# Another VectorE order at the ends of both attentions of a diffusion backbone, one latent projection between the last softmaxes, and the path weights rounded one block sooner

## Chip, cores and metric

One Trainium2 chip, one core. The metric is the device time of one launch in microseconds (us), the median of several runs. PE is TensorE, DVE is VectorE, ACT is ScalarE, POOL is GpSimd, and SP is the queue that starts nearly all loads.

## What is computed

Two layers (`DEPTH` = 2) over 640 tokens: 512 latent ones and 128 context ones, width 1024. The reference, cut to what matters here:

```
proj = h @ w_in[l]                    # hyena 1536, q k v 512 each, latent q 384, kv 256, kr 32, paths 1536, merge 3072
pr = softmax(s, -1); pr = pr[:, 0] - lam * pr[:, 1]          # differential attention (DA), 4 heads
y_da = rms_norm(pr @ v, da_subln) * (1 - lam_init)
c_q, c_kv = rms_norm(mla_dq), rms_norm(mla_dkv)              # the latent projections
y_mla = softmax(q k^T) v                                     # latent attention (ML), 8 heads
br = [y_hy, y_da, y_mla] * silu(paths)
merged = sum over the 3 branches of sigmoid(merge) * (br @ w_branch)
x = layer_norm(ALPHA * x + gate * (merged @ w_out))
```

## The kernel before

Everything runs in an order written by hand. `STEPS[l]` is one list of steps per layer, and every engine walks the same list and does its own part of each step, so each engine is in order. A step's result in PSUM goes to one of four slots of 1024 columns, dealt round in the order of the list. A step that takes a slot waits until the result that was in it, four slot uses earlier, has been read: those are the waits `freed`.

A *projection* is one step (`dqkv`, `path`, `mgate`, `v`, ...): a tile of 128 weight columns times all 640 tokens. The tile is split: ACT copies it from `W` to `Wh` (rounded, `high_part`), POOL, or for some tiles DVE, writes the rest into `Wl` (`low_part`), and PE runs 32 matmuls with `Wh` (lines 817 and 818) and 16 with `Wl` (822). `Wh` has two buffers, `W` has three. The table `UPTO` says at which step ACT and POOL do the rounding of a tile. With `near` true the tile that follows tile n is rounded at the start of tile n's own step, that is ahead of ACT's reading of tile n's result; with `near` false it is done at the next step, after that reading.

An attention is a run of units u = (head, block of 128 queries), five units a head, the fifth for the context tokens with a single block of 128 keys. For a unit PE computes scores (`da_score` into two slots, line 1073; `ml_score`, line 902 or 900), DVE takes the maximum (1525), ACT the exponential (1375 or 1449), DVE the normalised weights (`da_weights`, lines 1532 to 1535; `ml_weights`, 1552 and 1553). Two units later (`LAG` = 2) `ptrans` transposes the weights on PE (878), ACT copies them, and after a head's last unit `pv` multiplies with the values (923 and 924; 920 and 924 for ML). Weights of unit u-1 are written by DVE in the step `score` u, behind the maximum of unit u; those of an attention's last unit, in the step of the last `ptrans`. Projections are put between the units as *fillers*: here `mgate` d and `mbranch` d, at whose end DVE reads the result (1775, or 1778 and 1779).

After each DA head come `dasq` h (DVE squares the head's output, 1831), `dams` h (PE sums it over the 128 rows, 865; DVE scales the sum, 1836). After the last head `dart` (ACT square root, DVE reciprocal) and `dab` 0 to 3 (PE spreads the row, 873; DVE multiplies, 1845) finish the norm. The latent projections `dqkv` 0 to 4 stand among them; DVE squares each (1853), `mms` 0 sums the squares of the first three (865, DVE scales with 1871) and `mms` 1 the other two. The square of `dqkv` 3 overwrites that of `dqkv` 0, so DVE waits there for `mms` 0.

SP runs ahead of everybody as far as its waits let it. At step `dqkv` 3 it waits for the sum of the last head, since the weights that come next overwrite its input, then starts four loads of the latent attention and only then tile `dqkv` 3:

```
if (kind, i) == ("dqkv", 3):
    sp.wait_ge(*filled(l, "dams", 3))
    for dst, src in (wuq, wukv, cc, ckr):      # 1152, 1024, 128 and 16 KB
        sp.dma_start(dst, src)
...
weight(TILE_AT[l, kind, i] + n)                # 512 KB, waits for w_lo of the tile three before
```

Of the kernel before, what the change touches and what calls it, by code (L numbers as in the profile page):

```python
# [18 lines left out]
KD = D // 128  # L19
NT = NTOK // 128  # L20
# [3 lines left out]
DAH, DHD, DAV = 4, 64, 128  # L24
MH, MN, MR, MV = 8, 64, 32, 64
# [34 lines left out]
LAG = 2  # L60


def attention_steps(tag, heads, fillers, before=None, behind=None, full=False):


    steps, units, taken = [], [(h, t) for h in range(heads) for t in range(NT)], 0
    for u, (h, t) in enumerate(units):
        if before and h + 1 < heads:
            steps += before(h + 1, t)
        steps.append((tag + "_score", u))  # L70
        if u > LAG and (u - LAG - 1) % NT == NT - 1:
            steps.append((tag + "_pv", (u - LAG - 1) // NT))
        if behind and u > LAG + 1 and (u - LAG - 2) % NT == NT - 1:
            steps += behind((u - LAG - 2) // NT)[:1]
        if behind and u > LAG + 2 and (u - LAG - 3) % NT == NT - 1:
            steps += behind((u - LAG - 3) // NT)[1:]
        upto = min(t, 3) + 1 + 4 * h if full else len(fillers) * (u + 1) // len(units)
        steps += fillers[taken:upto]
        taken = upto
        if u >= LAG:  # L80
            steps.append((tag + "_ptrans", u - LAG))
    return steps + [(tag + "_ptrans", len(units) - LAG + n) for n in range(LAG)] + [(tag + "_pv", heads - 1)]


def path_steps(n):
# [3 lines left out]
def merge_steps(n):  # L89
    return [(kind, KD * n + d) for d in range(KD) for kind in ("mgate", "mbranch")]  # L90
# [47 lines left out]
def layer_steps(l):  # L138
# [25 lines left out]
        if c:  # L164
            s += [("vt", c - 1)]
    s += [("vt", 3)]
    s += attention_steps("da", DAH, merge_steps(0), behind=lambda h: [("dasq", h), ("dams", h)], full=True)
    s += [("dasq", 3), ("dqkv", 0), ("dams", 3), ("dqkv", 1), ("dart", 0), ("dqkv", 2)] + [("dab", h) for h in range(DAH)]
    s += [("dqkv", 3), ("mms", 0), ("dqkv", 4), ("kr", 0), ("mms", 1)]
    p = path_steps(1)  # L170
    s += p[:1] + [("mrt", 0)] + p[1:3] + [("mb", 0), ("mb", 1)] + p[3:] + [("cc", 0), ("sc", 0)]
    s += [("mv", i) for i in range(3)]
# [170 lines left out]
SLOT = slot_table()  # L343


def upto_table():


    table = {}
    for l in range(DEPTH):  # L350
        steps = [(n, step) for n, step in enumerate(STEPS[l]) if step[0] not in ("gmod", "nmod", "cload", "mload")]
        places = [n for n, (_, step) in enumerate(steps) if step in SPLIT_AT]
        table[l, STEPS[l].index(("ht", 0))] = 2
        for n, (a, b) in list(enumerate(zip(places, places[1:])))[1:]:
            near = b - a <= 2 or (SPLIT[n][0] == "conv" and b - a <= 3) or SPLIT[n] == ("qk", 0)
            table[l, steps[a if near else a + 1][0]] = n + 2
        table[l, STEPS[l].index(("inv", 4))] = SPLIT_AT["qk", 2] + 1
        early = SPLIT_AT["conv", 8]
        table[l, STEPS[l].index(("conv", 6))] = early + 1
    return table  # L360
# [62 lines left out]
def build(nc, A, O):  # L423
# [10 lines left out]
    with ctx:  # L434
# [189 lines left out]
        def after(name, l, count):  # L624

            return sems[name], l * PER[name] + count
# [6 lines left out]
        def filled(l, kind, i, j=0):  # L633

            s, u, _ = SLOT[l, kind, i, j]
            return full[s], u + 1
# [863 lines left out]
        def _(dve):  # L1500
# [27 lines left out]
            def da_weights(l, u):  # L1528

                n, s, e = keysn(u), st[:, u % (LAG + 1)], E[u % (LAG + 1)]  # L1530
                dve.wait_ge(*after("da_exp", l, 2 * u + 2))
                link(dve.reciprocal(s[:, 4:6], s[:, 2:4]))
                link(TT(s[:, 6:7], s[:, 5:6], lamc[:, 6:7], ALU.mult))
                link(TS(e[:, 0, 0:n], e[:, 0, 0:n], s[:, 4:5], None, ALU.mult))
                STT(e[:, 0, 0:n], e[:, 1, 0:n], s[:, 6:7], e[:, 0, 0:n], ALU.mult, ALU.add).then_inc(sems["da_p"], 1)
                dve.wait_ge(*own("da_p"))
# [48 lines left out]
            for l in range(DEPTH):  # L1585
                for kind, i in STEPS[l]:
# [9 lines left out]
                    elif kind in ("gmod", "nmod"):  # L1596
                        n = MODS[l].index((kind, i))
# [168 lines left out]
                    elif kind == "mbranch":  # L1766
                        n_, d = divmod(i, KD)
                        g = 12 * n_ + 4 + d
                        dve.wait_ge(*filled(l, kind, i))
                        ps = slot(l, kind, i)  # L1770
                        dve.wait_ge(*after("th_ready", l, g + 1))
# [46 lines left out]
                    elif kind == "da_score":  # L1818
# [5 lines left out]
                            dve.wait_ge(*own("da_max"))  # L1824
                        if i:
                            da_weights(l, i - 1)
                    elif kind == "da_ptrans" and i == DAH * NT - 1:
                        da_weights(l, i)
                    elif kind == "dasq":
                        dve.wait_ge(*after("da_o", l, i + 1))  # L1830
                        TT(sqd[:, i % 2], OT[:, i], OT[:, i], ALU.mult).then_inc(sems["da_sq"], 1)
# [46 lines left out]
                    elif kind == "mb":  # L1878
# [4 lines left out]
                        last.then_inc(sems["c_ready"], 1)  # L1883
                        dve.wait_ge(*own("c_ready"))
                    elif kind == "mqr":
                        dve.wait_ge(*after("mqr_raw", l, i + 1))
                        link(dve.stream_shuffle(qsw, rq, mask=[p ^ 8 for p in range(32)]))
                        TT(rq, rq, rope_m[:, 0], ALU.mult)
# [6 lines left out]
                    elif kind == "ml_score":  # L1895
                        dve.wait_ge(*filled(l, kind, i))
                        softmax_max(slot(l, kind, i), keysn(i), st[:, i % (LAG + 1), 0:1]).then_inc(sems["ml_max"], 1)
                        dve.wait_ge(*own("ml_max"))
                        if i:
                            ml_weights(l, i - 1)  # L1900
                    elif kind == "ml_ptrans" and i == MH * NT - 1:
                        ml_weights(l, i)
                    elif kind in ("xt", "xta", "xtb"):
                        dve.wait_ge(*filled(l, kind, i))
                        ps, blocks = slot(l, kind, i), BLOCKS[kind]
# [186 lines left out]
```

## Time and profile before

| | |
|---|---|
| median of 3 runs | 1925.25 us (1922.32 to 1926.27) |
| profiled execution | 1925.0 us, of it span 1923.2 us |
| PE busy (matmul) | 1802.9 us, 94% |
| DVE busy | 1125.5 us, 59% |
| ACT busy | 670.4 us, 35% |
| POOL busy | 451.7 us, 23% |
| chain that ended last | PE 66%, DVE 23%, issue 4%, ACT 4%, DMA 2%, POOL 1% |
| TensorE clock granted, mean | 0.983 of full speed |

Busy is the share of the span in which an engine executes; the chain is followed back from the last instruction to what released each one. A bracket behind a row of the timeline is the time the engine was idle ahead of it, and what ended that. Layer 0's DA ends near 490 us and its ML near 790 us; layer 1's, 938 us later.

### The profile page before, as it was taken

The numbers are of one execution on the slowest core, as the hardware profiler recorded it, in microseconds if no ns is written. First come the engines' busy times: TensorE is split into PE (matmuls) and PEld (weight loads), VectorE is DVE, ScalarE is ACT, GpSimd is POOL, SyncE is SP. The second block draws the span as 40 slices with busy tenths as digits, with TensorE's granted clock in tenths as the row PEclk, the third lists the DMA queues.
The fourth block names the chain that finished last, engine by engine and source line by source line (L and its number), as shares of the span: only waits on it lengthen the run. The fifth ranks groups of instructions, "written<-read, shape, count | busy, mean of one in ns | idle before, by whom it ended". The sixth has DMA issues, their size and how long they took to land.

```text
span 1923.2 us, 27833 instructions
## 1 busy us (share of the span) xinstructions
PE 1802.9 (94%) x11336; PEld 1572.3 (82%) x11336; DVE 1125.5 (59%) x1606; ACT 670.4 (35%) x1159; POOL 451.7 (23%) x208
## 2 busy tenths in 40 slices
PE   4999999999999999999989999999999999999997
PEld 3788799877786777899876969997879677779996
DVE  4689894445343444377877989925434343434755
ACT  3434312434234444321263342234433344442222
POOL 0100033222231111367300001322122211115561
PEclk8999999999999999999999999999999999999999
DMA  8111122211210111353621112221122011014431
GB/s 347 44 55 34 33 89 71 60 40 51 105 50 26 34 34 39 114 198 115 245 88 33 56 33 78 77 61 46 38 72 99 22 37 33 30 48 142 164 111 66
DMA packets 48622, 150.01 MB, mean 78 GB/s; under 512 B 9386, under 2 KB 11050, under 8 KB 47728
## 3 DMA queue, kind: packets, MB, share of 16 engines
q1 hardware_dynamic: 44896, 134.09, 20.3%
q10 hardware_dynamic: 3600, 14.16, 2.2%
q8 instruction: 90, 1.47, 0.3%
q14 instruction: 36, 0.29, 0.0%
HBM read 141.63 MB, written 6.59 MB: 77 GB/s over the span
## 4 chain that ended last, share of the span: by engine, by line
PE 66%; DVE 23%; issue 4%; ACT 4%; DMA 2%; POOL 1%; SPq 0%; ACTq 0%; DVEq 0%; POOLq 0%
PE PS L817 15%; PE PS L818 14%; PE PS L822 14%; PE PS L889 4%; PE PS L878 3%; PE PS L1140 2%; PE PS L923 2%; PE PS L920 2%; PE PS L1073 2%; PE PS L902 2%; DVE MG L1779 1%; DVE Wl L1546 1%; DVE st L1525 1%; DMA pmod_w<-in_w_mod 1%; PE PS L1129 1%
## 5 line engine op out<-in xcount | busy, mean ns | idle before, releaser
L1958 POOL TENSOR_TENSOR Wl<-W,Wh 128x1024 fp32r<-128x1024 f32 (+1 forms) x156 | 350.3, 2247 | 1291.9 <-ACT Wh L1193 1234.7
L817 PE MATMUL PS<-Hh,Wh 128*128 128x320 f32 x2048 | 613.5, 314 | 20.8 <-ACT Wh L1193 12.3
L818 PE MATMUL PS<-Hl,Wh 128*128 128x320 f32 x2048 | 604.9, 310 | 0.0
L817 PEld LDWEIGHTS PS<-Hh,Wh 128*128 128x128 f32 x2048 | 386.7, 189 | 45.9 <-issue 29.0
L818 PEld LDWEIGHTS PS<-Hl,Wh 128*128 128x128 f32 x2048 | 386.8, 189 | 0.6 <-issue 0.5
L822 PE MATMUL PS<-Hh,Wl 128*128 128x320 f32 x2048 | 321.4, 309 | 0.9 <-POOL Wl L1958 0.9
L822 PEld LDWEIGHTS PS<-Hh,Wl 128*128 128x128 f32 x2048 | 305.5, 188 | 1.5 <-POOL Wl L1958 1.5
L1525 DVE TENSOR_REDUCE st<-PS 128x1 f32<-128x640 f32 (+1 forms) x160 | 114.8, 718 | 315.1 <-PE PS L902 172.7
L1193 ACT ACTIVATE work<-PS 128x640 f32<-128x640 f32 (+9 forms) x298 | 172.6, 592 | 250.6 <-PE PS L822 64.2
L1193 ACT ACTIVATE Wh<-W 128x1024 fp32r<-128x1024 f32 (+1 forms) x188 | 176.4, 943 | 62.0 <-PE PS L822 26.8
L1350 ACT ACTIVATE th<-PS 128x640 f32<-128x640 f32 x64 | 45.1, 705 | 366.0 <-PE PS L822 366.0
L1193 ACT ACTIVATE raw<-PS 128x320 f32<-128x320 f32 (+4 forms) x98 | 38.1, 443 | 261.0 <-PE PS L822 188.6
L817 PE MATMUL PS<-BRh,Wh 128*128 128x320 f32 x384 | 116.4, 317 | 0.0
L818 PE MATMUL PS<-BRl,Wh 128*128 128x320 f32 x384 | 113.4, 309 | 0.0
L878 PE MATMUL PS<-fixed,work 128*128 128x128 f32 x580 | 88.5, 285 | 18.4 <-ACT work L1495 5.0
L878 PEld LDWEIGHTS PS<-fixed,work 128*128 128x128 f32 x580 | 72.7, 153 | 39.3 <-issue 12.8
L902 PE MATMUL PS<-work 96*128 96x320 f32 x256 | 81.0, 441 | 7.8 <-DVE MG L1779 4.5
L1604 DVE SCALAR_TENSOR_TENSOR raw<-work 128x1024 f32<-128x1024 f32 x46 | 82.4, 1792 | 7.6 <-DMA work<-in_w_mod_rows 6.1
L817 PEld LDWEIGHTS PS<-BRh,Wh 128*128 128x128 f32 x384 | 72.1, 188 | 7.0 <-ACT Wh L1193 6.1
L1375 ACT ACTIVATE work<-PS,st 128x640 f32<-128x640 f32 (+1 forms) x80 | 56.7, 710 | 55.7 <-DVE st L1525 55.7
L818 PEld LDWEIGHTS PS<-BRl,Wh 128*128 128x128 f32 x384 | 72.2, 188 | 0.0
L889 PE MATMUL PS<-work,MG 128*128 128x512 f32 x160 | 70.8, 594 | 1.0 <-ACT raw L1193 0.6
(234 smaller groups left out, 2502.8 us busy)
## 6 DMA issues: line engine op xcount, KB each, us to landing
W<-in_w_in SPq DMA_DIRECT2D x132, 512.0 KB, 3.5
W<-in_w_branch SPq DMA_DIRECT2D x48, 256.0 KB, 2.6
work<-in_w_mod_rows ACTq DMA_DIRECT2D x23, 512.0 KB, 3.7
pmod_w<-in_w_mod SPq DMA_DIRECT2D x8, 1024.0 KB, 14.4
W<-in_w_out SPq DMA_DIRECT2D x16, 512.0 KB, 4.5
work<-in_x_sample SPq DMA_DIRECT2D x2, 2048.0 KB
late_modulation_w<-in_w_mod_rows SPq DMA_DIRECT2D x5, 512.0 KB, 6.6
x_mid<-work SPq DMA_DIRECT2D x1, 2560.0 KB, 8.5
```

The lines of the kernel that those rows point to most:

```text
L817: pe.matmul(out, Wh[:, b, kk, :], xh[:, kk, t], start=kk == 0, stop=False)
L818: pe.matmul(out, Wh[:, b, kk, :], xl[:, kk, t], start=False, stop=False)
L822: last = pe.matmul(out, Wl[:, b, kk, :], xh[:, kk, t], start=False, stop=kk == k - 1)
L878: return pe.transpose(out, in_, ident[0:p, 0:p])
L889: last = pe.matmul(ps[:, 512 * q:512 * q + HY], table, srcs[q ^ c][:, r, :], start=n_ == 0, stop=n_ == len(terms) - 1)
L902: last = pe.matmul(ps[:, 512 * a:512 * a + HALF], q_lat[:, 128 * t:128 * t + 128], k[:, HALF * a:HALF * a + HALF], start=True, stop=True)
L1193: return act.activation(out, in_, ACT.Copy, scale=scale)
L1350: act.activation(halves(th[:, n % 2]), two(ps), ACT.Tanh, scale=0.5)\
L1375: act.activation(two_or_one(e, n), two(ps) if n > CTX else ps[:, 0:n], ACT.Exp, bias=st[:, i % (LAG + 1), j:j + 1], accum_out=st[:, i % (L ...
L1525: return dve.tensor_reduce(out, two(ps) if n > CTX else ps[:, 0:n], mybir.AxisListType.XY if n > CTX else AX, ALU.max, negate=True)
L1604: ins = STT(mod_early if n < EARLY[l] else mod_late, modw[mod_buffer(l, n)], scale, cb[:, j], ALU.mult, ALU.mult, accum_out=modcs[:, at_ % ...
L1958: return pool.tensor_tensor(out, in_, high.bitcast(f32), ALU.subtract)
```

## The change

Five edits. (1) In DA, `dasq` h goes behind the filler of its unit, and `dams` h one unit later, behind that unit's score. (2) `cover`: `dqkv` 0, and `dams` 2 behind it, go between the third-last and the second-last `ptrans` of DA; every later `dqkv` moves up by one place, and `dqkv` 3 and `mms` 0 go ahead of the four `dab`. (3) DVE writes the weights of DA's last unit in the last `score` step. (4) In ML, DVE writes the last unit's weights ahead of `mbranch` 15, and those of unit 14 ahead of the rotation of the second group of queries (`mqr` 1). (5) `early_high` makes `near` true for `path` 4 to 7, `dqkv` 0 and `dqkv` 3. The number of instructions of each engine is the same.

```
-        if behind and u > LAG + 1 and (u - LAG - 2) % NT == NT - 1:
-            steps += behind((u - LAG - 2) // NT)[:1]
-        if behind and u > LAG + 2 and (u - LAG - 3) % NT == NT - 1:
-            steps += behind((u - LAG - 3) // NT)[1:]
+        if behind and u > LAG + 3 and (u - LAG - 4) % NT == NT - 1:
+            steps += behind((u - LAG - 4) // NT)[1:]
         upto = min(t, 3) + 1 + 4 * h if full else len(fillers) * (u + 1) // len(units)
         steps += fillers[taken:upto]
         taken = upto
+        if behind and u > LAG + 1 and (u - LAG - 2) % NT == NT - 1:
+            steps += behind((u - LAG - 2) // NT)[:1]
         if u >= LAG:
             steps.append((tag + "_ptrans", u - LAG))
-    return steps + [(tag + "_ptrans", len(units) - LAG + n) for n in range(LAG)] + [(tag + "_pv", heads - 1)]
+    return steps + list(cover) + [(tag + "_ptrans", len(units) - LAG + n) for n in range(LAG)] + [(tag + "_pv", heads - 1)]
...
-    s += attention_steps("da", DAH, merge_steps(0), behind=lambda h: [("dasq", h), ("dams", h)], full=True)
-    s += [("dasq", 3), ("dqkv", 0), ("dams", 3), ("dqkv", 1), ("dart", 0), ("dqkv", 2)] + [("dab", h) for h in range(DAH)]
-    s += [("dqkv", 3), ("mms", 0), ("dqkv", 4), ("kr", 0), ("mms", 1)]
+    s += attention_steps("da", DAH, merge_steps(0), behind=lambda h: [("dasq", h), ("dams", h)], full=True,
+                         cover=[("dqkv", 0), ("dams", 2)])
+    s += [("dasq", 3), ("dqkv", 1), ("dams", 3), ("dqkv", 2), ("dart", 0), ("dqkv", 3), ("mms", 0)] + [("dab", h) for h in range(DAH)]
+    s += [ ("dqkv", 4), ("kr", 0), ("mms", 1)]
...
+def early_high(tile):
+    return tile[0] == "path" and 4 <= tile[1] < 8 or tile in (("dqkv", 0), ("dqkv", 3))
...
-            near = b - a <= 2 or (SPLIT[n][0] == "conv" and b - a <= 3) or SPLIT[n] == ("qk", 0)
+            near = b - a <= 2 or (SPLIT[n][0] == "conv" and b - a <= 3) or SPLIT[n] == ("qk", 0) or early_high(SPLIT[n])
...
                     elif kind == "mbranch":
+                        if i == 2 * KD - 1:
+                            ml_weights(l, MH * NT - 1)
...
-                    elif kind == "da_ptrans" and i == DAH * NT - 1:
-                        da_weights(l, i)
+                        if i == DAH * NT - 1:
+                            da_weights(l, i)
...
                     elif kind == "mqr":
+                        if i:
+                            ml_weights(l, 3 * NT - 1)
...
-                        if i:
+                        if i and i != 3 * NT:
                             ml_weights(l, i - 1)
-                    elif kind == "ml_ptrans" and i == MH * NT - 1:
-                        ml_weights(l, i)
```

DVE at the border of two DA heads: `MG` is the reading of `mbranch`, the row `work<-work 128x640` on line 1831 (1839 in the changed kernel) is `dasq`, `raw<-PS` is `dams`. Before:

```order
L1535 SCALAR_TENSOR_TENSOR work<-work,st 128x640
L1831 TENSOR_TENSOR work<-work 128x640
L1775 SCALAR_TENSOR_TENSOR MG<-th,PS 128x640
L1525 TENSOR_REDUCE st<-PS 128x1 x2
L1532 RECIPROCAL st<-st 128x2
L1533 TENSOR_TENSOR st<-st,small 128x1
L1534 TENSOR_SCALAR work<-work,st 128x640
L1535 SCALAR_TENSOR_TENSOR work<-work,st 128x640
L1836 TENSOR_SCALAR raw<-PS 64x320
L1525 TENSOR_REDUCE st<-PS 128x1 x2
```

And with the change:

```order
L1541 SCALAR_TENSOR_TENSOR work<-work,st 128x640
L1783 SCALAR_TENSOR_TENSOR MG<-th,PS 128x640
L1839 TENSOR_TENSOR work<-work 128x640
L1531 TENSOR_REDUCE st<-PS 128x1 x2
L1538 RECIPROCAL st<-st 128x2
L1539 TENSOR_TENSOR st<-st,small 128x1
L1540 TENSOR_SCALAR work<-work,st 128x640
L1541 SCALAR_TENSOR_TENSOR work<-work,st 128x640
L1531 TENSOR_REDUCE st<-PS 128x1 x2
```

The square and the reading of the filler have changed places, and the scaling has left the place between two softmax units; it now follows the weights of the next unit.

ACT from the end of DA on. `Wh_56<-W_55 128x1024` is the rounding of a tile, `work_76<-PS` with a number is the copy of a result (640 columns wide: of `pv` 3 or of a `dqkv`), the table load and `raw_63` are the square root of `dart`. Before, from the copy of `pv` 3:

```order
L1193 ACTIVATE work_76<-PS2 128x640
L1193 ACTIVATE Wh_56<-W_55 128x1024
L1193 ACTIVATE work_76<-PS3 128x640
L1193 ACTIVATE Wh_56<-W_55 128x1024
L1193 ACTIVATE work_76<-PS1 128x640
L1395 ACT_TABLE_LOAD
L1395 ACTIVATE raw_63<-raw_63 128x640
L1193 ACTIVATE work_76<-PS2 128x640
L1193 ACTIVATE Wh_56<-W_55 128x1024 x2
L1193 ACTIVATE work_76<-PS3 128x640
```

With the change, from the same copy:

```order
L1199 ACTIVATE work_76<-PS3 128x640
L1199 ACTIVATE Wh_56<-W_55 128x1024
L1199 ACTIVATE work_76<-PS0 128x640
L1199 ACTIVATE Wh_56<-W_55 128x1024
L1199 ACTIVATE work_76<-PS2 128x640
L1401 ACT_TABLE_LOAD
L1401 ACTIVATE raw_63<-raw_63 128x640
L1199 ACTIVATE Wh_56<-W_55 128x1024
L1199 ACTIVATE work_76<-PS3 128x640
```

The results copied between the roundings were `dqkv` 0, 1, 2, 3 and are now `dqkv` 1, 2, 3; the second rounding shown is of tile `dqkv` 2 before and of tile `dqkv` 3 now, and it stands ahead of the copy of `dqkv` 2 and of the square root.

DVE at the end of ML, where `th<-th,PS` and `MG<-MG,th` are the reading of `mbranch` 15. Before:

```order
L1552 RECIPROCAL st<-st 128x1
L1553 TENSOR_SCALAR raw<-raw,st 128x640
L1778 SCALAR_TENSOR_TENSOR th<-th,PS 128x640
L1779 TENSOR_TENSOR MG<-MG,th 128x640
L1552 RECIPROCAL st<-st 128x1
L1553 TENSOR_SCALAR work<-work,st 128x128
```

With the change:

```order
L1558 RECIPROCAL st<-st 128x1
L1559 TENSOR_SCALAR raw<-raw,st 128x640
L1558 RECIPROCAL st<-st 128x1
L1559 TENSOR_SCALAR work<-work,st 128x128
L1786 SCALAR_TENSOR_TENSOR th<-th,PS 128x640
L1787 TENSOR_TENSOR MG<-MG,th 128x640
```

The two instructions that write the last unit's weights now come ahead of the filler's result.

## Rows read from the trace of the kernel before

**Rows 1.** What PE waited for, whole span: total us, times, longest

```profile
PE PS L865 <- DVE MG L1775: 4.6, 6, 0.8
...
PE PS L878 <- DVE work L1553: 4.2, 2, 2.1
```

**Rows 2.** Timeline, border of DA heads 2 and 3: start, us, work [idle before]

```profile
442.29 0.37 ACT L1375 ACTIVATE work<-PS,st 128x128 f32<-128x128 f32 x1 [0.81 <-DVE st L1525]
...
443.28 1.35 PE L1073 MATMUL PS<-work 64*128 64x320 f32 x8
...
445.44 0.38 PE L817 MATMUL PS<-Hh,Wh 128*128 128x320 f32 x1 [0.81 <-DVE raw L1836]
```

**Rows 3.** Timeline of PE and ACT, end of DA, layer 0

```profile
459.56 4.56 PE L923 MATMUL PS<-work 128*128 128x512 f32 x10
...
477.39 0.49 PE L1073 MATMUL PS<-work 64*128 64x128 f32 x4
...
481.54 0.77 PE L878 MATMUL PS<-fixed,work 128*128 128x128 f32 x5 [1.46 <-DVE work L1535]
...
482.34 0.70 ACT L1193 ACTIVATE work<-PS 128x640 f32<-128x640 f32 x1 [1.52 <-PE PS L878]
...
483.53 0.28 ACT L1193 ACTIVATE work<-PS 128x128 f32<-128x128 f32 x1 [0.48 <-PE PS L878]
...
483.86 6.19 PE L923 MATMUL PS<-work 128*128 128x512 f32 x10 [0.37 <-ACT work L1193]
...
490.03 0.39 PE L817 MATMUL PS<-Hh,Wh 128*128 128x320 f32 x1
...
497.24 0.73 PE L865 MATMUL PS<-work,fixed 128*32 128x320 f32 x4
```

**Rows 4.** Timeline of SP, layer 0, as it passes the wait at `dqkv` 3

```profile
498.01 0.38 SPq L759 DMA_DIRECT2D work<-in_mla_w_uq  x1
...
500.18 0.46 SPq L675 DMA_DIRECT2D W<-in_w_in  x1
```

**Rows 5.** That tile's DMA, layer 0, then layer 1: size, us from issue to landing

```profile
W<-in_w_in SPq DMA_DIRECT2D x1, 512.0 KB, 8.7
...
W<-in_w_in SPq DMA_DIRECT2D x1, 512.0 KB, 7.5
```

**Rows 6.** Timeline from the four `dab` to `mms` 0, layer 0

```profile
513.94 1.80 DVE L1845 SCALAR_TENSOR_TENSOR work<-work,small,PS 128x640 f32<-128x640 f32 x2
...
514.97 0.61 PE L817 MATMUL PS<-Hh,Wh 128*128 128x320 f32 x1 [1.10 <-ACT Wh L1193]
...
523.50 1.81 PE L865 MATMUL PS<-work,fixed 128*32 128x320 f32 x12
```

**Rows 7.** Timeline around `path` 7 and the values of ML, layer 0

```profile
563.84 0.42 PE L817 MATMUL PS<-Hh,Wh 128*128 128x320 f32 x1 [0.99 <-ACT Wh L1193]
...
569.26 2.61 PE L822 MATMUL PS<-Hh,Wl 128*128 128x320 f32 x16 [0.47 <-POOL Wl L1958]
...
572.51 1.05 ACT L1193 ACTIVATE Wh<-W 128x1024 fp32r<-128x1024 f32 x1
...
574.33 10.57 PE L1129 MATMUL PS<-work 128*128 128x512 f32 x24 [1.74 <-ACT work L1193]
```

**Rows 8.** Timeline of PE, ML: `mqn` 2 behind `ptrans` 14, then `pv` 7 in both layers

```profile
669.20 3.51 PE L1140 MATMUL PS<-work 128*128 128x512 f32 x12
...
788.47 2.38 PE L920 MATMUL PS<-work 128*64 128x256 f32 x20 [0.37 <-ACT work L1193]
...
1727.02 3.65 PE L920 MATMUL PS<-work 128*64 128x256 f32 x20 [0.37 <-ACT work L1193]
```

**Rows 9.** Stretches: busy us of PE, PEld, DVE, ACT, POOL, then granted clock

```profile
484.00:490.00 6.00, 6.00 (x12) 2.62 (x13) 0.00 (x0) 0.00 (x0) 0.00 (x0) 0.74 0.00 0
...
981.00:986.00 5.00, 4.42 (x21) 4.21 (x22) 2.09 (x4) 2.22 (x5) 0.00 (x0) 0.55 0.78 328
```

**Rows 10.** Timeline of PE, start of layer 1: the longest wait inside the span

```profile
981.56 4.30 PE L878 MATMUL PS<-fixed,work 128*128 128x128 f32 x20 [5.03 <-ACT work L1495]
```

More of the change, by code:

```diff
@@ L60, with attention_steps @@
 LAG = 2
-def attention_steps(tag, heads, fillers, before=None, behind=None, full=False):
+def attention_steps(tag, heads, fillers, before=None, behind=None, full=False, cover=()):
     steps, units, taken = [], [(h, t) for h in range(heads) for t in range(NT)], 0
```

## The prediction

> **What bounds the kernel now.** I read the shares first, then the waits of PE, then the timeline at each place that the diff touches. PE is busy 1802.9 of 1923.2 us, so all other waits together leave it idle some 120 us, and the chain that ended last lies on PE for 66% and on DVE for 23%. No instruction is removed. What can change is only when PE stands still, and at which of its two clock levels it works. The waits of PE list the places: `dams` (line 865) waited six times, 4.6 us in all, for DVE's reading of a filler, and the single transpose of a context unit's weights twice, 2.1 us at the longest [rows 1]. The timeline shows the rest: at a DA border `mgate` waits 0.81 us for the scaling of `dams` [rows 2]; at the end of DA PE stands 1.46, then 0.85, then 0.37 us between transposes and values (the 0.85 is what is left between the rows at 481.54 and 483.86), and the ten value matmuls that follow take 6.19 us where the same ten took 4.56 a head earlier [rows 3]. The granted clock of that stretch is 0.74 [rows 9], part of it at 1.2 GHz in place of 2.4: the chain of short waits is paid for a second time by 1.6 us of slow matmuls. `dqkv` 3 has 1.10 us ahead of it [rows 6], `path` 7 has 0.99 and 0.47, the values of ML 1.74 [rows 7], the last `pv` of ML 2.11 and 0.37 [rows 1, 8].
>
> **Part 1: the borders of DA heads (edit 1).** Twice a layer, `dams` 0 and 1. Before, PE lost 0.77 (4.6 over six) ahead of `dams` and 0.81 ahead of `mgate`, 1.58 together [rows 1, 2]. With the change, DVE reads the filler 0.8 us sooner and both these waits are gone. But the slots are dealt anew: the next score (443.28 before) now takes the slot of the context unit's first score, and waits for its exponential, which ACT begins at 442.29, since DVE still does square and maximum in the old time, and which takes 0.4 [rows 2]. PE is ready for that score at about 441.9 (`ptrans` comes in `dams`' place), so it stands 0.9. Score 443.28 becomes 442.8, `dams` follows it (0.65), `mgate` starts at 444.7 in place of 445.44: 0.7 saved, four times: **2.8 us**. Bounds: nothing, if the exponential comes later still by 0.7, and 6.3, if there is no new wait. I take 2.8, because each time in it is a row's.
>
> **Part 2: the end of DA (edits 2, 3, 5).** I follow layer 0. The last score ends at 477.9. Before, `dqkv` 0 started at 490.03 and `dams` 3 at 497.24, so a projection costs 7.2 [rows 3]. Now: `ptrans` 17 to 478.5, `dqkv` 0 to 485.7, under which DVE writes both last units' weights. `dams` 2 and `ptrans` 18 (0.7 each) to 487.1, `ptrans` 19 under ACT's copy, the two copies (0.70, 0.28) to 488.2. The values take 4.5 at full clock, since the one wait left is some 0.8, to 492.7. With `dqkv` 0 done, that is 4.5 ahead of before (497.24). `dqkv` 1 ends at 499.9, `dams` 3 at 500.6.
>
> Here the gain meets SP. Its wait at `dqkv` 3 ended with `dams` 3, at 498.01, and the tile of `dqkv` 3 was issued at 500.18, behind four loads of 2.3 MB [rows 4]. It landed 8.7 us later in layer 0 and 7.5 in layer 1 [rows 5], which is 10.9 us after `dams` 3 (508.9) and, with the same 2.2 us of issue, 9.7 in layer 1. Before, that was hidden: between `dams` 3 and `dqkv` 3 PE had two projections and the spreads, and came to `dqkv` 3 at 514.97 [rows 6]. Now only one projection stands there, `dqkv` 2. It ends at 507.8. The tile lands at 511.5, ACT rounds it and PE starts 1.1 later (the row's wait for `Wh`, nearly all of it the 1.05 of the rounding [rows 6, 7]) at 512.6: **a new wait of 4.8 us, in layer 1 of 3.6.** No edit touches SP's order; rounding earlier can't help a tile that isn't there. Queued behind the rounding on ACT stand the copy of `dqkv` 2 and the square root of `dart`, then the reciprocal on DVE; they are done before PE has finished `dqkv` 3, so I cost them at nothing.
>
> After such a wait PE works slowly. The row for it is the start of layer 1: 5.03 us idle, and then a mean clock of 0.55 over five us [rows 9, 10], some 4.5 us at 1.2 GHz, which cost 2.2. The short waits at the end of DA cost 1.6. I take 1.7, near the short one, since the wait is as long as that row's but PE was in full work up to it: `dqkv` 3 runs 512.6 to 521.5, `mms` 0 (1.81) to 523.3. DVE then does square of `dqkv` 3, scaling of `mms` 0 and the first `dab`: three instructions, the last 0.9 [rows 6], 2.2 together (2.7 at most), before the slots for `dab` 3 and `dqkv` 4 are free. `dqkv` 4 starts at 525.5, before it was 523.50 + 1.81 = 525.3 [rows 6]. So layer 0 loses 0.2, and layer 1, with 1.2 less of a wait, wins 1.0: **0.8 us** for the whole part, nearly all of it eaten. Bounds: if the tile isn't waited for, `dqkv` 3 runs 507.8 to 515.0, `dqkv` 4 starts at 519.0, and the part gives 6.3 a layer, 12.6. If the clock drops a second time at the small waits around `dab`, it gives 0.8 - 2 x (1.5 + 0.3), or -2.8.
>
> A page of the Trainium skill gives another price for the loads. DMA: Bandwidth & Descriptors (Where 436 GB/s comes from; Latency and other measured facts) puts the limit into SBUF near 435 GB/s and a fixed cost near 2 us. The five loads are 2.9 MB, by that page an estimate of 6.7 + 2 = 8.7 us, where the rows show 10.9 and 9.7. By the page the wait would be 2.6 in both layers and the sum 3.2 better. The rows decide: the issue alone takes 2.2 us of it, and they differ by layer.
>
> **Part 3: paths (edit 5).** `path` 6 is followed by the spreads `mb`, so the tile of `path` 7 was rounded only after `path` 6 was read. Now ACT does it under `path` 6, and POOL does `Wl` ahead of the low part of the branch; both waits, 0.99 and 0.47, go. `path` 7 likewise hands its place to `mgate` 8: the rounding (1.05) leaves the gap of 1.74 ahead of the values of ML, 0.7 stays [rows 7]. That is 2.5 a layer, **5.0 us**. All inputs are early: the tiles land a projection or more ahead. Bounds: 2.1 (only the middle one of these edits' waits, 1.05, goes in each layer) and 5.5.
>
> **Part 4: ML (edit 4).** At `mqr` 1 the transpose of unit 14 no longer waits 1.7 us. But the next on PE, `mqn` 2, starts at 669.20 in the slot of unit 15's scores [rows 8], just as their exponential ends, and its maximum stands behind the same rotation as before. PE comes to it earlier and waits longer: **nothing**. At the end of ML the weights of unit 39 fall into time in which DVE waited for the filler. The last transpose follows at once and its wait of 2.11 goes, but its copy now queues on ACT behind those of the two transposes ahead, some 0.4 by the 0.70 of such a copy [rows 1, 3]: 1.7 in layer 0. In layer 1 the same, and `pv` 7 took 3.65 there in place of 2.38 [rows 8]; I count that the slow clock goes with the wait, 1.3: 3.0. Sum **4.7 us**; bounds 3.4 (clock stays) and 5.
>
> **Sum.** 2.8 + 0.8 + 5.0 + 4.7 = 13.3 us off the profiled execution's 1925.0, that is 1911.7. The median of the runs is 1925.25, 0.25 above it: **1912 us**, 0.7% faster.
>
> **Rivals.** (a) *The loads are hidden anyway.* For it: the tile's landing differs by 1.2 us between the layers, and 0.5 MB alone would come sooner. Against: SP is one queue and the four loads stand ahead in code. Then part 2 gives 12.6 and the time is 1925.25 - 25.1 = 1900. Chance 0.15. (b) *The loads go at the page's rate* (the wait is 2.6 twice): 1912 - 3.2 = 1909. The rule is that of the DMA page above. Chance 0.08; traces don't bear it out. (c) *The clock takes more.* Two drops a layer, part 2 at -2.8, and part 1 gives nothing: 13.3 - 3.6 - 2.8 = 6.9, 1918. For it: one wait of five us, then spreads of one row with two waits of half a us, just where PE ran slowly in the trace of before. Chance 0.14. TensorE: Matmul & The Clock Gate (HAM oscillation) describes this: a wait for a DMA in the middle of a loop puts the array back to the low clock, and the cost is half of the throttled time. (d) *The tile of `dqkv` 3 comes much later, and the kernel is slower.* Each us costs one in each layer, so it decides from 6.7 us on (a landing 17.6 after `dams` 3 in layer 0). At 8 later: 1912 + 16 = 1928. Against it, 10.9 and 9.7 in the rows. With anything else that ends above 1921: 0.06. (e) *The change does as the sum says*, 1907 to 1917: 0.57.
>
> **Range and chances.** 1900 to 1919 holds (e), (b), (c) and about half of (a); what is left out is (d), half of (a) and the far end of (c), 0.17. A measurement of this kernel tells about 0.2%, 3.9 us, from no change. Faster than 1921.4: 0.88. Within: 0.07. Slower: 0.05.
>
> **What would show it.** In the changed trace: PE's waits for DVE at line 865 and at the 1.46 and 0.85 gone; the first score of DA heads 2 and 3 waiting near 0.9 for ACT's exponential; the values of DA at 4.6 us; `dqkv` 3 waiting 4.8 and 3.6 us for `Wh`, with ACT waiting for the DMA of `W` ahead of it, and low clock behind; no wait at `path` 7, 0.7 at the values of ML; the transpose at `mqr` 1 without a wait and `mqn` 2 with 1.9; `pv` 7 of ML 1.7 sooner. I am wrong if `dqkv` 3 doesn't wait (then nearer 1900), or if PE's clock falls at other places too.

## The result, and the profile after

The changed kernel takes 1930.66 us (median of 5 runs, 1929.99 to 1932.94), the one before 1923.82 beside it (1922.32 to 1926.27): the ratio is 1.0037, 95% interval 1.0022 to 1.0051. That is 0.4% slower, where 1912 us, 0.7% faster, was forecast.

The profiled execution took 1932.48 us, its span 1930.7, 7.5 more than before. Two lines of the page after, the busy times and the chain's shares by engine:

```profile
PE 1805.9 (94%) x11336; PEld 1576.2 (82%) x11336; DVE 1138.2 (59%) x1606; ACT 668.8 (35%) x1159; POOL 447.1 (23%) x208
...
PE 69%; DVE 20%; ACT 4%; issue 3%; DMA 3%; SPq 0%; POOL 0%; ACTq 0%; DVEq 0%
```

DVE executes the same instructions as before and is busy 12.7 us longer (1125.5 before): some of them last longer. That is the first sign. The waits of PE after (total us, times, longest):

```profile
PE PS L823 <- ACT Wh L1199: 15.3, 12, 4.0
...
PE PS L1079 <- ACT work L1381: 9.8, 6, 2.3
...
PE PS L879 <- DVE work L1879: 4.7, 2, 2.3
...
PE PS L926 <- DVE MG L1787: 3.1, 2, 1.6
```

`dams` no longer waits for `MG` [rows 1]. In its place stand the score behind a context unit (line 1079, 2.3 us), tile `dqkv` 3 (line 823, 4.0), `dab` 3 (line 879, 2.3) and the last `pv` of ML (line 926, 1.6). The timeline of the changed kernel at the border that [rows 2] show of before:

```profile
443.37 2.35 POOL L1966 TENSOR_TENSOR Wl<-W,Wh 128x1024 fp32r<-128x1024 f32 x1 [3.00 <-PE PS L828]
443.40 0.82 DVE L1783 SCALAR_TENSOR_TENSOR MG<-th,PS 128x640 f32<-128x640 f32 x1
...
444.26 2.15 DVE L1839 TENSOR_TENSOR work<-work 128x640 f32<-128x640 f32 x1
...
446.44 0.62 DVE L1531 TENSOR_REDUCE st<-PS 128x1 f32<-128x128 f32 x2
446.82 0.37 ACT L1381 ACTIVATE work<-PS,st 128x128 f32<-128x128 f32 x1 [2.24 <-DVE st L1531]
...
447.42 1.35 PE L1079 MATMUL PS<-work 64*128 64x320 f32 x8 [2.32 <-ACT work L1381]
```

The square of `dasq` (line 1839) takes 2.15 us, and ends 0.7 after GpSimd's subtraction has ended (443.37 + 2.35 = 445.72). The reading of `mbranch` ahead of it (line 1783: one input in PSUM) lies under the same subtraction and takes its 0.82. The maximum, the exponential and the score all come behind the square. And the timeline of the same square and subtraction before:

```profile
440.19 0.82 DVE L1831 TENSOR_TENSOR work<-work 128x640 f32<-128x640 f32 x1
440.26 2.97 POOL L1958 TENSOR_TENSOR Wl<-W,Wh 128x1024 fp32r<-128x1024 f32 x1 [2.99 <-PE PS L822]
...
525.34 2.41 POOL L1958 TENSOR_TENSOR Wl<-W,Wh 128x1024 fp32r<-128x1024 f32 x1 [6.62 <-ACT Wh L1193]
525.46 2.96 DVE L1853 TENSOR_TENSOR work<-work 128x640 f32<-128x640 f32 x1 [7.88 <-PE PS L865]
```

There the square of `dasq` began 0.07 us ahead of the subtraction and it was GpSimd that took 2.97 in place of 2.4. The other pair shows the reverse: the square of `dqkv` 3 began 0.12 behind GpSimd and took 2.96. So the trace of before held both cases, and the prediction read neither.

The end of DA in the changed kernel, tile `dqkv` 3 and then the `dab`, layer 0:

```profile
504.57 0.38 SPq L765 DMA_DIRECT2D work<-in_mla_w_uq  x1
...
506.77 1.43 SPq L681 DMA_DIRECT2D W<-in_w_in  x3
...
514.15 1.06 ACT L1199 ACTIVATE Wh<-W 128x1024 fp32r<-128x1024 f32 x1 [9.54 <-DMA W<-in_w_in]
...
515.26 0.64 PE L823 MATMUL PS<-Hh,Wh 128*128 128x320 f32 x1 [3.50 <-ACT Wh L1199]
...
526.78 2.34 POOL L1966 TENSOR_TENSOR Wl<-W,Wh 128x1024 fp32r<-128x1024 f32 x1 [5.54 <-ACT Wh L1199]
526.91 2.90 DVE L1861 TENSOR_TENSOR work<-work 128x640 f32<-128x640 f32 x1 [4.39 <-PE PS L871]
529.84 0.48 DVE L1879 TENSOR_SCALAR work<-PS 64x320 f32<-64x320 f32 x1
...
530.37 0.88 PE L879 MATMUL PS<-raw,fixed 1*128 1x320 f32 x4 [2.34 <-DVE work L1879]
```

The forecast wait for the late tile is there, 3.50 us (4.8 forecast) and 3.96 in layer 1 (3.6). Behind it comes a second one: `dab` 3 needs the slot that DVE frees with the scaling of `mms` 0, and that stands behind a square of 2.90 us. Windows of the changed kernel (PEclk, third from the right, is the mean granted clock) over the borders and the end of DA in both layers:

```profile
400.00:550.00 150.00, 138.24 (x838) 116.04 (x835) 70.53 (x104) 52.17 (x95) 33.64 (x17) 0.95 0.19 68
1340.00:1480.00 140.00, 127.90 (x749) 105.83 (x750) 67.63 (x99) 48.31 (x92) 30.07 (x15) 0.93 0.20 68
```

and of the kernel before:

```profile
400.00:550.00 150.00, 142.16 (x885) 120.63 (x884) 68.95 (x111) 54.10 (x96) 36.34 (x17) 0.98 0.20 71
1340.00:1480.00 140.00, 132.16 (x815) 110.50 (x814) 61.15 (x100) 50.10 (x92) 33.38 (x16) 0.98 0.21 72
```

A mean of 1.00 is 2.4 GHz and one of 0.50 is 1.2 GHz, so in layer 1 the mean of 0.93 over 140 us is 2 x 0.07 x 140 = 20 us at 1.2 GHz, where 0.98 was 6. The clock fell behind most of the new waits, but not behind each. Windows of the changed kernel, first in layer 0 and then in layer 1: behind the score's wait at one of the two borders, and behind the wait for tile `dqkv` 3:

```profile
447.00:451.00 4.00, 3.58 (x23) 2.56 (x24) 3.72 (x9) 2.31 (x8) 0.00 (x0) 1.00 0.14 53
514.00:521.00 7.00, 5.74 (x22) 5.75 (x23) 5.07 (x2) 4.61 (x5) 4.50 (x2) 0.52 0.50 186
...
1350.00:1354.00 4.00, 4.00 (x18) 2.62 (x15) 3.64 (x8) 1.74 (x4) 0.00 (x0) 0.57 0.02 4
1456.00:1463.00 7.00, 5.15 (x20) 5.15 (x21) 4.48 (x2) 4.61 (x5) 3.91 (x2) 0.51 0.53 198
```

The other two borders have 0.57 (408 to 412) and 0.61 (1388 to 1392), and behind the `dab` 3 wait it is 0.58 (531 to 535) and 0.51 (1473 to 1480). The same score, after the same 2.32 us, kept the full clock in one place of four. `mqn` 2 of ML shows it once more, 12 matmuls behind a wait of 2.07 us, in layer 0 and in layer 1 (timeline of the changed kernel):

```profile
673.94 5.21 PE L1146 MATMUL PS<-work 128*128 128x512 f32 x12 [2.07 <-ACT work L1455]
...
1617.77 3.51 PE L1146 MATMUL PS<-work 128*128 128x512 f32 x12 [2.07 <-ACT work L1455]
```

So the length of a wait of some 2 us does not tell here whether the clock falls behind it; what decides that, no run here shows.

**The theory** is then two causes, each with its share of the clock: (i) VectorE instructions such as the square, with both inputs in SBUF, that begin while GpSimd subtracts are held until it ends; (ii) the tile of `dqkv` 3 is late. The rivals: the redealt slots or the clock alone; and that the parts of the change harm or feed each other. The Trainium skill, page SBUF — State Buffer (SBUF: two separate sides), states (i) as a rule: a VectorE instruction in a two-port mode, or one with two inputs in SBUF while GpSimd's instruction reads SBUF, and the GpSimd instruction exclude one another for the whole length of whichever began first. The rows agree in both directions: VectorE's 0.82 us became 2.96, and GpSimd's 2.4 became 2.97.

### The profile page after: what moved, and what is told of

Its sections match the earlier page's. It is cut to its first block, busy times and chain, and to the rows that moved or that the text cites. A ratio compares the mean times of both kernels' runs of the same rounds, so it can differ in the third digit from the quotient of the medians.

```text
span 1930.7 us, 27833 instructions
## 1 busy us (share of the span) xinstructions
PE 1805.9 (94%) x11336; PEld 1576.2 (82%) x11336; DVE 1138.2 (59%) x1606; ACT 668.8 (35%) x1159; POOL 447.1 (23%) x208
## 4 chain that ended last, share of the span: by engine, by line
PE 69%; DVE 20%; ACT 4%; issue 3%; DMA 3%; SPq 0%; POOL 0%; ACTq 0%; DVEq 0%
PE PS L823 15%; PE PS L824 15%; PE PS L828 14%; PE PS L895 4%; PE PS L884 3%; PE PS L1079 2%; PE PS L1146 2%; PE PS L926 2%; PE PS L929 2%; PE PS L908 2%; DMA pmod_w<-in_w_mod 1%; DVE MG L1787 1%; DVE Wl L1552 1%; PE PS L1135 1%; PE PS L1154 1%
## 5 line engine op out<-in xcount | busy, mean ns | idle before, releaser
L1966 POOL TENSOR_TENSOR Wl<-W,Wh 128x1024 fp32r<-128x1024 f32 (+1 forms) x156 | 345.7, 2217 | 1312.6 <-ACT Wh L1199 1255.4
L823 PE MATMUL PS<-Hh,Wh 128*128 128x320 f32 x2048 | 618.2, 316 | 20.8 <-ACT Wh L1199 15.3
```

Of the source, the lines that this page charges most:

```text
L823: pe.matmul(out, Wh[:, b, kk, :], xh[:, kk, t], start=kk == 0, stop=False)
L1966: return pool.tensor_tensor(out, in_, high.bitcast(f32), ALU.subtract)
```

## The experiments

Each time is the median of 4 to 11 runs; the kernel before took 1923.9 to 1924.4 us beside them. "Less than the changed kernel" is against its 1930.66.

**The parts alone: r1, r2, r3.** The kernel before, with edits 4 and 5 (path 4 to 7) alone:

```
-            near = ... or SPLIT[n] == ("qk", 0)
+            near = ... or SPLIT[n] == ("qk", 0) or SPLIT[n][0] == "path" and 4 <= SPLIT[n][1] < 8
+                        if i == 2 * KD - 1:
+                            ml_weights(l, MH * NT - 1)      # and the other lines of edit 4
```

> The kernel before with the path and ML edits alone (4, and 5 for path 4 to 7). Theory A (the loss sits in the DA edits, these two parts pay as their rows after the change show): 2.7 us a layer at the paths, 1.2 and 2.6 at the ends of ML, 9.2 us off: 1914.7 us against 1923.8. Rival B (the gain at the paths is there only because PE comes late to them from the DA end, and is given back when it does not): 3 us off or less, 1921 or more.

Measured: 1913.18 us (1912.69 to 1915.01), ratio 0.9944 (0.9932 to 0.9957), 10.8 off. These parts pay on their own, 1.6 more than the 9.2 that was expected; rival B of this run falls.

With edit 1, and `dams` 2 moved as in edit 2:

```
-        if behind and u > LAG + 2 and (u - LAG - 3) % NT == NT - 1:
-            steps += behind((u - LAG - 3) // NT)[1:]
+        if behind and u > LAG + 3 and (u - LAG - 4) % NT == NT - 1:
+            steps += behind((u - LAG - 4) // NT)[1:]       # and dasq behind the filler
```

> The kernel before with edit 1 alone (square behind the filler, scaling of dams one unit later; dams 2 in front of ptrans 18). Theory A (the square starts under GpSimd's subtraction for Wl and is held by it: 2.1 us in place of 0.82, the score behind it waits 2.3 us, and the clock falls at some of these places): the two changes of head in each layer lose 2 us each, 7.8 us in all, 1931.6. Rival B (the borders gain the 0.7 each that the prediction gave, and the loss seen there comes from other edits, through the slots dealt anew): 2.8 us off, 1921. Rival C (only the clock): the waits are 0.9 as predicted and drops of 3.4 us cost about 1.7 each at some of them, within 3 us of before.

Measured: 1934.23 us (1932.95 to 1934.96), ratio 1.0052 (1.0038 to 1.0065), 10.3 slower, where 7.8 was expected. The score's waits for the exponential are the same 9.8 us in six; rivals B and C of this run fall. But this is more than the borders. `dams` 2 stands here ahead of the second-last `ptrans` without the `dqkv` 0 that covers it in the full change, and PE waits for `dasq` 2, again a square held to 2.15 us, in both layers:

```profile
485.15 0.73 PE L865 MATMUL PS<-work,fixed 128*32 128x320 f32 x4 [1.44 <-DVE work L1831]
```

These 2.9 us, with their share of the clock (a mean of 0.72 from 484 to 496), are of this run alone, so the borders cost less than 10.3.

With edits 2 (without `dams` 2) and 3, and 5 for `dqkv` 0 and 3:

```
+    s += attention_steps(..., cover=[("dqkv", 0)])
+    s += [("dasq", 3), ("dqkv", 1), ("dams", 3), ("dqkv", 2), ("dart", 0), ("dqkv", 3), ("mms", 0)] + [dab 0 to 3] + [("dqkv", 4), ...
```

> The kernel before with edits 2 and 3, and 5 for the two latent tiles, alone. Theory A (dqkv 3's tile is late by 3.5 and 4.0 us, the clock falls behind it, and the square ahead of dab is held by GpSimd's subtraction): 3.5 us slower in layer 0 and 5.0 in layer 1, 8.5 in all, 1932.3. Rival B (this part's loss is brought on by the later dams of edit 1): the part gives the 0.8 us of the prediction, 1923.

Measured: 1932.41 us (1932.23 to 1935.83), ratio 1.0050 (1.0037 to 1.0062), 8.5 slower. The three add up to 8.0 slower; the whole change measured 6.8, and r2 has 2.9 us of waits that it has not. Nothing here asks for parts that harm or feed each other.

**The late tile: r4 and r9.** The changed kernel, with the tile issued ahead of SP's wait, and then behind the wait but ahead of the loads (in both it is no longer issued at its old place):

```
 if (kind, i) == ("dqkv", 3):
+    weight(TILE_AT[l, kind, i])          # r4
     sp.wait_ge(*filled(l, "dams", 3))
+    weight(TILE_AT[l, kind, i])          # r9, in place of r4's
     for dst, src in (wuq, wukv, cc, ckr):
```

> The changed kernel, with SP issuing the tile of dqkv 3 ahead of its wait for dams 3 and of the four latent loads. Theory A: the waits of dqkv 3 for Wh (3.50 and 3.96 us) are gone, and with them most of the low clock behind them (3.4 us of it gives 1.7 back in each layer): 9 to 11 us less than the changed kernel, about 1921. Rival B (the tile comes as late whatever its place, since the queue or its buffer holds it): the waits stay and the time is 1930.7. If the square ahead of dab and the wait of 2.34 us behind it are the larger part, the clock still falls there: 1923 to 1925.

> The changed kernel, with the tile of dqkv 3 issued behind SP's wait for dams 3 but ahead of the four latent loads. Theory A (the four loads in front, not the wait itself, make it late: alone it would land some 3.5 us after its issue at 504.6, near 508, three us ahead of the end of dqkv 2): no wait at dqkv 3, as when it stands ahead of the wait too, 1919 to 1920. Rival B (the loads that follow share the same DMA engines and delay it anyway): it lands at 511 to 513 and dqkv 3 still waits 1 to 3 us, 1923 to 1928.

Measured: r4 1919.33 us (1913.25 to 1922.49), ratio 0.9975 (0.9965 to 0.9985), 11.3 less than the changed kernel; r9 1920.79 us (1918.52 to 1922.09), 0.9982 (0.9973 to 0.9991). Neither waits for the tile: 6.8 us in nine waits for `Wh` are left in both, of the 15.3 in twelve. In r9 SP's timeline reads:

```profile
503.15 0.33 SPq L681 DMA_DIRECT2D W<-in_w_in  x1
503.52 0.44 SPq L766 DMA_DIRECT2D work<-in_mla_w_uq  x1
```

and the row of that tile in its DMA view (KB, us from issue to landing):

```profile
W<-in_w_in SPq DMA_DIRECT2D x1, 512.0 KB, 3.4
```

It took 3.4 us with the four loads behind it, and 7.4 in the changed kernel with them in front. The wait on `dams` 3 cost nothing that these runs can tell; the place behind 2.3 MB did.

**The square at the borders: r5 and r6.** Two ways to part the square from the subtraction. In r5 VectorE's order is changed back; in r6 it is left alone, and only ScalarE's and GpSimd's rounding moves:

```
+        if behind and u > LAG + 1 and (u - LAG - 2) % NT == NT - 1:      # r5: dasq ahead of the filler
+            steps += behind((u - LAG - 2) // NT)[:1]
+            later = 4 if SPLIT[n] in (("mbranch", 3), ("mbranch", 5)) else 1      # r6
+            table[l, steps[a if near else a + later][0]] = n + 2
```

> The changed kernel with dasq put back ahead of the filler, as before; dams stays one unit later. Theory A (a square that starts while GpSimd subtracts is held until GpSimd has done): the square starts ahead of the subtraction and takes 0.82 us instead of 2.1, the score behind it waits about 0.9 instead of 2.3, the drops of the clock there go: 5.6 us from the four waits and up to 5 from the clock, 1920 to 1925. Rival B (the score waits for the exponential's slot, whatever the square takes): its wait stays above 2 us, and the time stays at 1930.

> The changed kernel with VectorE's order untouched; ScalarE and GpSimd do the rounding of the tiles behind mbranch 3 and mbranch 5 three steps later, so that no subtraction lies under the square. Theory A (GpSimd holds the square): the same VectorE order now gives a square of 0.82 us and a score that waits 0.9; unless the later tile is missed by its own projection, 1920 to 1925. Rival B (the square is slow because of what stands ahead of it on VectorE, or because of its operands): it still takes 2.1 us and the score still waits 2.3.

Measured: r5 1921.13 us (1920.1 to 1922.89), ratio 0.9984 (0.9975 to 0.9993), 9.5 less than the changed kernel; r6 1918.8 us (1917.85 to 1921.32), 0.9976 (0.9967 to 0.9985), 11.9 less. The timeline of r6 at the border:

```profile
441.92 0.83 DVE L1840 TENSOR_TENSOR work<-work 128x640 f32<-128x640 f32 x1
...
443.77 1.35 PE L1080 MATMUL PS<-work 64*128 64x320 f32 x8 [1.00 <-ACT work L1382]
...
445.00 2.55 POOL L1967 TENSOR_TENSOR Wl<-W,Wh 128x1024 fp32r<-128x1024 f32 x1 [6.96 <-ACT Wh L1200]
```

The same VectorE instruction in the same order, with the same operands: 0.83 us once GpSimd works later. The score waits 1.00; the prediction had 0.9. That shows (i), and rules out the order and the slots. In r5 each border starts its next `mgate` 0.6 us sooner than before, four times; the prediction had 0.7.

**The square ahead of the `dab`: r7.** r4 with one more move (the added line in words):

```
 elif kind == "dqkv":     # VectorE
-    if i == 3: dve.wait_ge(*filled(l, "mms", 0))
-    square of dqkv i
+    i < 3: square of dqkv i;  i == 3: nothing;  i == 4: squares of dqkv 3 and 4
```

> The kernel of r4_tile_first, with VectorE's square of dqkv 3 moved from ahead of the scaling of mms 0 and the four dab to the step of dqkv 4 (behind them). Theory A (that square, held for 2.9 us by GpSimd's subtraction, is what dab 3 waits for and what lets the clock fall there): the wait of 2.34 us at the dab goes in both layers, the low clock behind it too: 7 to 9 us less than 1919.3, 1910 to 1912. Rival B (the scaling and the dab themselves are what is late, the clock falls anyway): 2 to 4 us less, 1915 to 1917.

Measured: 1908.15 us (1906.81 to 1911.1), ratio 0.9919 (0.9906 to 0.9933), 11.2 less than r4. Its timeline:

```profile
521.70 2.36 POOL L1966 TENSOR_TENSOR Wl<-W,Wh 128x1024 fp32r<-128x1024 f32 x1 [2.56 <-ACT Wh L1200]
521.79 0.48 DVE L1879 TENSOR_SCALAR work<-PS 64x320 f32<-64x320 f32 x1 [1.85 <-PE PS L872]
...
523.56 0.39 PE L824 MATMUL PS<-Hh,Wh 128*128 128x320 f32 x1 [0.42 <-DVE work L1854]
```

The scaling reads PSUM and isn't held by the subtraction that it lies under. The wait of 2.34 us at `dab` 3 is gone; `dqkv` 4 waits 0.42 for a `dab`. I expected 7 to 9 us and it gave 11.2, but not all of that is this wait's. The edit doesn't touch the borders, where the score waits 2.32 us in r4 and in r7 alike, and still the clock differs. Windows over the two borders of layer 1 in r4:

```profile
1340.00:1400.00 60.00, 55.16 (x323) 44.78 (x324) 30.51 (x55) 23.62 (x50) 10.35 (x6) 0.91 0.12 39
```

and in r7:

```profile
1325.00:1385.00 60.00, 55.16 (x354) 46.49 (x353) 31.30 (x55) 23.95 (x50) 10.89 (x6) 1.00 0.12 40
```

That is 2 x 0.09 x 60 = 11 us at the low clock, some 5 us of time, that r7's profiled execution had not and that its edit doesn't explain. The runs of r4 themselves go from 1913.25 us (mean granted clock 0.987) to 1922.49 (0.982). So the wait is shown; how much of the 11.2 hung on it stays open.

**All repairs: r8.** r7 with r5's order.

> The changed kernel with all three repairs: dasq ahead of the filler, the tile of dqkv 3 ahead of the four loads, and the square of dqkv 3 behind the dab. If the three losses are separate they add up: 11.3 for the tile, 8 for the dab, 6 to 10 for the borders, 1902 to 1906. If a repaired place only hands its wait on to the next one, it stays above 1910.

Measured: 1899.7 us (1897.77 to 1901.34), ratio 0.9873 (0.9859 to 0.9886). From the changed kernel that is 31.0 less; the single steps are 11.3 + 11.2 + 9.5 = 32.0. The same windows of r8:

```profile
400.00:550.00 150.00, 145.87 (x933) 125.90 (x933) 73.24 (x115) 58.05 (x101) 40.39 (x19) 1.00 0.21 73
1340.00:1480.00 140.00, 136.87 (x873) 118.50 (x872) 63.47 (x95) 51.51 (x86) 37.86 (x18) 1.00 0.21 72
```

No drop of the clock is left there in this execution.

**The last `pv` of ML: r10.** r8, with the slot of `mbranch` 15 freed by the instruction that reads it (the added line is shortened):

```
-    "mbranch": [("gate_used", ...)]
+    "mbranch": [("mb_read", 1) if i == 15 else ("gate_used", ...)]
...
-    link(STT(halves(t_), halves(t_), 1.0, two(ps), ALU.add, ALU.mult))
+    read = STT(...);  i == 15: read.then_inc(sems["mb_read"], 1)
     TT(m, m, t_, ALU.add).then_inc(sems["gate_used"], 1)
```

> The kernel of r8_best1; the slot in which the result of mbranch 15 lies is freed by VectorE's first instruction (the one that reads it) and no longer by the second (the addition to MG). Theory A (pv 7 of ML waits 1.57 us for that slot alone): the wait shrinks by the 0.8 us or more of the addition in both layers, 1.5 to 3 us less than 1899.7. Rival B (it would wait as long for the copy of the last transpose): nothing, 1899.7.

Measured: 1897.24 us (1896.63 to 1899.11), ratio 0.9863 (0.9847 to 0.9879), 2.5 less than r8. The two ranges overlap, so it is the row that carries this reading. The row of `pv` 7 in r8:

```profile
777.48 2.38 PE L927 MATMUL PS<-work 128*64 128x256 f32 x20 [1.57 <-DVE MG L1788]
```

and in r10:

```profile
777.32 1.67 DVE L1793 TENSOR_TENSOR MG<-MG,th 128x640 f32<-128x640 f32 x1
...
778.48 2.38 PE L927 MATMUL PS<-work 128*64 128x256 f32 x20 [0.90 <-ACT work L1200]
```

The slot's wait of 1.57 is gone; 0.90 is left for the copy of the last transpose. The addition itself takes 1.67, again under a subtraction (GpSimd, 775.96 to 778.32).

**Two that failed: r11 and r12.** From (i) I inferred that all additions to `MG` between the units of ML should be moved out of the subtraction:

```
+            later = 2 if SPLIT[n][0] == "mbranch" and 8 <= SPLIT[n][1] < 16 else 1      # r12: 3
+            table[l, steps[a if near else a + later][0]] = n + 2
```

> The kernel of r10_best2; the rounding (ScalarE, and so GpSimd's subtraction) of the tile behind each mbranch 8 to 15, between the units of ML, comes one step later. Theory A (the addition to MG takes 1.4 or 1.67 us in place of 0.82 because it starts under GpSimd's subtraction, and the next score waits for it, 12 times, 4.5 us in all): where the later rounding gets the subtraction behind the addition, the addition takes 0.82 and those waits go, up to 4.5 us less than 1897.2. Rival B (GpSimd's start isn't moved enough, or the exponential comes later behind the rounding on ScalarE, and the next transposes wait for it): no gain, or slower by up to 1 us for each of 16 tiles.

> As r11_ml_round_2, with the rounding two steps later. Theory A: all additions outside the subtraction, 0.82 us, 4.5 us less than 1897.2. Rival B: the tile's rounding is late for its own projection or moves the exponential: no gain or slower. If the first of the two is faster and this one not, ScalarE's place decides.

Measured: r11 1916.73 us (1916.48 to 1918.22), ratio 0.9966; r12 1911.04 us (1908.43 to 1912.62), ratio 0.9931: 19.5 and 13.8 slower than r10. The timeline of r11:

```profile
631.60 0.82 DVE L1794 TENSOR_TENSOR MG<-MG,th 128x640 f32<-128x640 f32 x1
...
632.96 2.34 POOL L1972 TENSOR_TENSOR Wl<-W,Wh 128x1024 fp32r<-128x1024 f32 x1 [8.21 <-ACT Wh L1201]
...
633.51 1.87 DVE L1561 TENSOR_SCALAR work<-work,st 128x128 f32<-128x128 f32 x1
...
635.44 0.33 PE L886 MATMUL PS<-fixed,work 128*128 128x128 f32 x1 [1.54 <-DVE work L1561]
```

and the longest waits of r12:

```profile
PE PS L928 <- ACT work L1201: 12.8, 10, 1.8
PE PS L1148 <- ACT work L1457: 8.5, 2, 4.2
```

The additions between the units take 0.82 in both, as (i) says. But in r11 the subtraction now holds the writing of the weights (1.87 in place of 0.29), on which the next transpose waits, ten times 15.4 us in all, where r10 had twelve waits of 4.5 us in all. In r12 ScalarE comes late, with the copies ahead of `pv` (12.8 us of waits, 4.2 in r10) and the exponential ahead of `mqn` 2 (8.5, 4.1 in r10). The subtraction lay in the cheapest of these three places already.

## Why the prediction was wrong

**Part 1, the borders (forecast 2.8 faster; with the square put right the changed kernel gains 9.5 in r5 and 11.9 in r6).** The step that failed is "since DVE still does square and maximum in the old time". Its count of waits and slots was right: with the square at 0.83, r6 has the score's wait at 1.00 and r5 wins 0.6 a border. But behind the filler the square begins 0.9 us into GpSimd's subtraction and ends 1.3 later; the wait is 2.32 in place of 0.9. Four times 1.4 make a loss of 2.9 out of the 2.8 gained, and behind three of the four waits the clock fell as well, for which the part had no term. The bound "nothing, if the exponential comes later still by 0.7" stopped at zero; 1.4 later was outside it.

**Part 2, the end of DA (forecast 0.8 faster; alone 8.5 slower).** The cover works as said: the values take 4.56 us, the old waits are gone. The tile's wait was forecast with the right cause and nearly the right size. Two terms failed. "three instructions, the last 0.9 [rows 6], 2.2 together (2.7 at most)" has the square at its free duration; the row of before that shows it at 2.96, on the same instruction, was not read, and that alone is more than the bound. And the clock: 1.7 a layer for one drop, where it is at 0.52 and 0.51 for 7 us behind the tile and falls again at the `dab`. The second drop was the bound at -2.8, and rival (c); it came. With both waits repaired (r4, r7) 22.5 us come back. Of these the waits are 3.50 + 3.96 + 2 x 2.34 = 12.1; most of the rest is low clock, and part of that, as r7 shows, lay at the borders.

**Parts 3 and 4 (forecast 5.0 and 4.7; together alone 10.8).** Right in the main. `path` 7 has no wait, the values of ML 0.8 (0.7 forecast), `mqn` 2 waits 2.07 (1.9). That this longer wait costs "nothing" had no term for the clock: in layer 0 of the changed kernel it fell there, 5.21 us in place of 3.51, in layer 1 and in r1 it did not. At the end of ML 1.2 and 2.6 were won of 1.7 and 3.0: "The last transpose follows at once" left out that the slot of `pv` 7 is that of `mbranch` 15, and so waits for both of DVE's instructions there (r10).

**The sum.** Waits that it hadn't are 4 x 1.4 and 2 x 2.34, 10.3 us. The low clock in the two windows is some 35 us (2 x 0.05 x 150 and 2 x 0.07 x 140) where the kernel before had 12, which at half speed is about 11 us more, and the forecast had it nearly unchanged (1.6 a layer gone, 1.7 new). That is an estimate of 21 us from these rows, for the 18.7 between 1912 and 1930.66.

**The rivals.** (a), (b), (c) and (e) all forecast a gain. (d), at 0.06, held all that ends above 1921, and named the late tile alone; the squares cost more than the tile (r5 to r7 against r4). The sign "if PE's clock falls at other places too" came. Rival (b) took the rate of the Trainium skill's page (DMA: Bandwidth & Descriptors, Where 436 GB/s comes from), an estimate of 8.7 us for the loads: the tile landed 9.6 us after `dams` 3 in layer 0, between that and the row's 10.9, and 10.0 after it in layer 1, where the row had 9.7.

## What to carry to other kernels

Before an instruction of VectorE is moved, look at what GpSimd does at the place that it leaves and at the place that it comes to: list the durations of one instruction over the whole trace, and where one is longer, see what ran beside it. Before a step is moved ahead of a queue's wait, look how many bytes stand in front of what it needs, and issue the small urgent load first. A wait of 2 us between full work can cost the clock too, in one execution and not in the next: give it a term and a range. Here r4 and r7 gave 22.5 us for 12.1 us of waits, and r11 cost 19.5 for about 18 us of waits more.

## What the runs showed of the hardware

A VectorE instruction with both inputs in SBUF (squares, additions, 128x640) that begins under GpSimd's subtraction ends 0.7 us after it: 2.15, 2.43, 2.90 by how much of it was left, against 0.82 when free. A float32 one from SBUF to SBUF with a factor (128x128, 0.29 when free) is held too and ends 0.1 us after it: 1.87 in r11, and 2.35 in the changed kernel:

```profile
486.85 2.41 POOL L1966 TENSOR_TENSOR Wl<-W,Wh 128x1024 fp32r<-128x1024 f32 x1 [3.52 <-ACT Wh L1199]
486.99 2.35 DVE L1540 TENSOR_SCALAR work<-work,st 128x128 f32<-128x128 f32 x1
```

When VectorE begins first, GpSimd's 2.4 becomes 2.97. VectorE instructions with an input in PSUM aren't held (0.82 at 443.40, 0.48 at 521.79). Nor is every one held that reads only SBUF: the reciprocal of `dart` (128x640) takes 4.15 us in the changed kernel with a whole subtraction of 2.38 inside it (518.87), and 4.15 in the kernel before with none. That the cause is a port is the word of the Trainium skill's page, SBUF — State Buffer (SBUF: two separate sides); the runs show the exclusion in time.
